# The down projection of a decoder layer in seven products of quarters, with GpSimd forming the operand sums

## The reference, cut to what matters

```python
h2 = _rmsnorm(x, g_pre_ffn)
ffn = (jax.nn.silu(h2 @ w_gate) * (h2 @ w_up)) @ w_down      # (1032, 2816) @ (2816, 1024)
x = x + _rmsnorm(ffn, g_post_ffn)
```

## Time and profile before

| | us |
|---|---|
| median of 3 runs | 1290.61 (1289.73 to 1292.06) |
| the profiled execution | 1288.78 |
| its span, first to last instruction | 1286.9 |
| TensorE busy | 1244.6 |
| VectorE busy | 838.0 |
| ScalarE busy | 465.4 |
| GpSimd busy | 37.2 |

### The profile page before, as it was taken

One profiled execution on the slowest core, in us unless ns is written; L12 is line 12 of the kernel. 1 busy time (PEld: TensorE's weight loads), 2 busy tenths in 40 slices (PEclk: granted clock), 3 DMA queues, 4 the chain that ended last, 5 costly groups with the idle time before them and its releaser, 6 DMA issues.

```text
span 1286.9 us, 22506 instructions
## 1 busy us (share of the span) xinstructions
PE 1244.6 (97%) x9161; PEld 1221.6 (95%) x9161; DVE 838.0 (65%) x1476; ACT 465.4 (36%) x910; POOL 37.2 (3%) x52
## 2 busy tenths in 40 slices
...
GB/s 290 102 70 50 33 19 2 42 11 85 17 69 49 101 110 121 67 98 138 94 108 94 128 54 87 65 94 99 50 88 79 150 330 176 117 251 180 103 274 109
DMA packets 141877, 135.29 MB, mean 105 GB/s; under 512 B 15976, under 2 KB 124792, under 8 KB 141248
## 3 DMA queue, kind: packets, MB, share of 16 engines
...
## 4 chain that ended last, share of the span: by engine, by line
PE 57%; DVE 8%; issue 1%; ACT 1%; DMA 0%; POOL 0%; POOLq 0%; DVEq 0%; ACTq 0%
PE pair L1495 32%; PE pair L1533 16%; PE pair L1454 5%; PE pair L1224 1%; DVE w_lo L2113 1%; DVE mix L1963 1%; PE pair L1353 1%; DVE mix L1988 1%; DVE w_lo L1921 1%; DVE qinv L1959 1%; DMA raw<-w_down_dram 0%; PE pair L1420 0%; DVE yo L2134 0%; POOL yo L840 0%; ACT w_hi L846 0%
## 5 line engine op out<-in xcount | busy, mean ns | idle before, releaser
L1495 PE MATMUL pair<-act_hi,w_hi 128*128 128x258 f32 x704 | 199.6, 284 | 4.3 <-DVE w_lo L1921 2.8
L1495 PE MATMUL pair<-act_hi,w_lo 128*128 128x258 f32 x704 | 198.9, 283 | 0.0
L1495 PE MATMUL pair<-act_lo,w_hi 128*128 128x258 f32 x704 | 198.8, 282 | 0.0
L1224 PE MATMUL pair<-act_hi,w_hi 128*128 128x344 f32 x528 | 180.4, 342 | 6.4 <-DVE act_lo L1586 3.5
L1533 PE MATMUL pair<-h_hi,w_hi 128*128 128x400 f32 (+1 forms) x528 | 170.4, 323 | 1.7 <-DVE h_lo L2116 1.7
L1224 PE MATMUL pair<-act_hi,w_lo 128*128 128x344 f32 x528 | 171.6, 325 | 0.0
L1224 PE MATMUL pair<-act_lo,w_hi 128*128 128x344 f32 x528 | 171.5, 325 | 0.0
L1533 PE MATMUL pair<-h_hi,w_lo 128*128 128x400 f32 (+1 forms) x528 | 170.0, 322 | 0.0
L1533 PE MATMUL pair<-h_lo,w_hi 128*128 128x400 f32 (+1 forms) x528 | 169.8, 322 | 0.0
L1495 PE MATMUL pair<-s_hi,w_lo 128*128 128x258 f32 x528 | 149.3, 283 | 0.0
L1495 PE MATMUL pair<-s_hi,w_hi 128*128 128x258 f32 x528 | 149.2, 283 | 0.0
...
## 6 DMA issues: line engine op xcount, KB each, us to landing
...
hraw<-h_scratch SPq DMA_DIRECT2D x44, 200.0 KB, 4.0
...
```

What stands on the lines that cost most here:

```text
L1224: mm = pe.matmul(out, a[:, k, :], b[:, k, cols(c)], start=(k == 0 and s == 0), stop=(k == KT - 1 and s == 2))
L1495: mm = pe.matmul(pair[psum_pair(n)][:, s, 0:QW], a[:, r, half + k, :], b, start=(k == 0 and i == 0), stop=(k == 3 and i == 2))
```

## The change

The down projection becomes seven products M1 to M7, each of half the rows (516), half the inner width (11 tiles) and half the output width (512), in the order M3, M1, M7, M5, M4, M2, M6 (`DOWN`). `A_OF` and `B_OF` say which quarters of h and of w_down are added or subtracted for each. Their outputs are added into the four quarters of the output.

A step loads, sums, splits and multiplies one inner tile: 4 output tiles x 2 blocks of 258 rows x 3 matmuls. All eight banks belong to each product, two per output tile (`dpair`). M6 runs its two row blocks one after the other, so it has 22 half-steps of 12 matmuls.

The four quarters h11, h22, w11 and w22 stay on chip after their first load, and so does w12 + w11, formed in M4 and split there and in M6's first steps (`TURN_AT`). In M3 a step loads h11, w12 and w22 (770 KB), in M1 h22 and w11, in M7 h12 and w21, in M5 h12, in M4 w21 and w12, in M2 h21, in M6 the half row block of h21. The loads wait as before for the split three before; M6 has six input slots.

The operand sums are GpSimd's (`sum_b`, `sum_a`), and so are most residual sums (`add_x2`, two tiles of 258 columns at once). In the tail GpSimd adds the residual to 5 of 8 tiles and VectorE to 3. Products are taken out of PSUM by copies on ScalarE (`y_copy`) and by copies and adds on VectorE (`y_first`, `y_add`), `y_add` having one operand in PSUM, one in SBUF. The wait for the stores of h to land goes from SyncE's queue to `holes_stored` on ScalarE and VectorE.

The core of the diff; the removed lines of the functions printed above are left out:

```diff
-DCH = ((0, 400), (400, 400), (800, 232))
 DR, DH = 3, 4
-HELD = 3
+HELD = 4
+POOL_TAIL = 5
+ADD, SUB = ALU.add, ALU.subtract
+DOWN = ("M3", "M1", "M7", "M5", "M4", "M2", "M6")
+A_OF = {"M1": ("11", "22", ADD), "M2": ("21", "22", ADD), "M3": ("11",), "M4": ("22",), "M5": ("12", "11", ADD),
+        "M6": ("21", "11", SUB), "M7": ("12", "22", SUB)}
+B_OF = {"M1": ("11", "22", ADD), "M2": ("11",), "M3": ("12", "22", SUB), "M4": ("21", "11", SUB), "M5": ("22",),
+        "M7": ("21", "22", ADD)}
+STEPS = [(p, m) for p in DOWN[:-1] for m in range(HALVES)] + [("M6", m) for _ in range(2) for m in range(HALVES)]
+FULL = (len(DOWN) - 1) * HALVES
+AT = {p: HALVES * i for i, p in enumerate(DOWN)}
+TURN_AT = {AT["M4"] + 3 + m if m < 8 else FULL + m - 8: m for m in range(HALVES)}
...
+    a_ring, _ = at("a_ring", [P, DH, 2, HALF], F32R, region)
+    b_ring = [(w_hi[:, (2 + n) % 4, 0:4].rearrange("p k n -> p (k n)"), w_lo[:, (2 + n) % 4, 0:4].rearrange("p k n -> p (k n)"))
+              for n in range(DH)]
...
+    b_in = [rawx[:, i // 2, 4 * (i % 2):4 * (i % 2) + 4].rearrange("p k n -> p (k n)") for i in range(DR)]
...
+    HALF_SLOT = [max(v for v in range(FULL) if v % DH == n) for n in range(DH)]
+    def a_free(v):
+        if v < DH:
+            return prod_used("P6" if v < 2 else "P7")
+        if v < FULL:
+            return step_used(v - DH)
+        h = v - FULL
+        return step_used(v - 2 * DH) if h >= 2 * DH else step_used(HALF_SLOT[h // 2])
...
+        def load_a(v):
+            p, m = STEPS[v]
+            slot, name = a_slot(v)
+            if p == "M4":
+                return
+            if v >= FULL + DR and v < FULL + 2 * DR:
+                sp.wait_ge(sem("d_split"), FULL)
+            elif v >= FULL + 2 * DR:
+                sp.wait_ge(sem("h_split"), v - 2 * DR + 1)
+            elif v >= DR:
+                sp.wait_ge(sem("h_split"), v - DR + 1)
+            if p == "M3":
+                sp.wait_ge(*prod_used("P1" if m < 4 else "P2" if m < 8 else "P5"))
+                load_h(a11(m), m, "11", name)
+            elif p == "M1":
+                load_h(a22(m), m, "22", name)
+            elif p == "M6":
+                load_h(slot, m, "21", name, slice(QW * sub(v), QW * sub(v) + QW))
+            else:
+                load_h(slot, m, A_OF[p][0], name)
...
+        for v in range(DR, NSTEP):
+            if v == AT["M1"]:
+                sp.wait_ge(sem("prod"), NPROD)
+                sp.wait_ge(sem("hid"), HIDDEN_AT["21", FT - 1])
+            load_a(v)
+            if v < FULL:
+                load_w(v)
+            k = v - (AT["M2"] + DR + 1)
+            if 0 <= k < KT:
+                sp.wait_ge(sem("a_sum"), a_sums(AT["M2"] + k + (k >= 4)))
+                sp.dma_start(x2a(k, 1)[:, 0], x2_d[:, k, HALF:ROWS]).then_inc(sem("x2_in"), 16)
+            if v == FULL + 10:
+                sp.wait_ge(sem("x2_in"), 16 * KT)
+                sp.wait_ge(sem("acc_mm"), 4 * (len(DOWN) - 1))
+                for k in range(0, KT, 4):
+                    sp.dma_start(x2b[:, k:k + 4], x2_d[:, k:k + 4, 0:HALF]).then_inc(sem("x2_in"), 16)
+            if v == FULL + 14:
+                for k in range(0, KT, 2):
+                    sp.wait_ge(sem("y_done_p"), KT // 2 + k // 2 + 1)
+                    sp.dma_start(t_out["y_cols"][:, k:k + 2, HALF:ROWS], yo[:, k:k + 2, HALF:ROWS]).then_inc(sem("y_out"), 16)
...
+        def sum_b(v):
+            p, m = STEPS[v]
+            if not b_summed(v):
+                return
+            pool.wait_ge(sem(B_SEM[v % DR]), b_count[v])
+            x = b_in[v % DR]
+            if p == "M1":
+                pool.wait_ge(sem("d_split"), v - DR + 1)
+                pool.tensor_tensor(x, b11(m), b22(m), ADD).then_inc(sem("b_sum"), 1)
+                return
+            if p == "M4":
+                pool.tensor_tensor(t_in32[:, m], t_in32[:, m], b11(m), ADD)
+            y = b11(m) if B_OF[p][1] == "11" else b22(m)
+            pool.tensor_tensor(x, x, y, B_OF[p][2]).then_inc(sem("b_sum"), 1)
+        def sum_a(v):
+            p, m = STEPS[v]
+            if not a_summed(v):
+                return
+            x, name = a_slot(v)
+            pool.wait_ge(sem(name), a_count[v])
+            if p == "M1":
+                pool.wait_ge(sem(f"rows_in{m % DR}"), a_count[m])
+                pool.wait_ge(sem("h_split"), v - DR + 1)
+                pool.tensor_tensor(x, a11(m), a22(m), ADD).then_inc(sem("a_sum"), 1)
+                return
+            y = a11(m) if A_OF[p][1] == "11" else a22(m)
+            pool.tensor_tensor(x, x, own(y, v), A_OF[p][2]).then_inc(sem("a_sum"), 1)
+        def add_x2(b, k, n=2):
+            rows = block_rows(b)
+            x = yo[:, k:k + n, rows]
+            r = QW * (b % 2)
+            y = x2a(k, n)[:, :, r:r + QW] if b < 2 else x2b[:, k:k + n, r:r + QW]
+            pool.wait_ge(sem("y_t"), KT * b + k + n)
+            pool.tensor_tensor(x, x, y, ADD).then_inc(sem("y_done_p"), 1)
+        for v in range(NSTEP):
+            if v == AT["M1"]:
+                pool.wait_ge(sem("hid"), HIDDEN_AT["21", FT - 1])
+            if v < FULL:
+                sum_b(v)
+            sum_a(v)
+            n = v - (FULL - 3)
+            if 0 <= n < 8:
+                if n == 0:
+                    pool.wait_ge(sem("x2_in"), 16 * KT)
+                add_x2(n // 4, 2 * (n % 4))
+        pool.wait_ge(sem("x2_in"), 16 * (KT + 2))
+        for k in range(0, KT, 2):
+            add_x2(2, k)
+        for k in range(POOL_TAIL):
+            add_x2(3, k, 1)
...
         def down_hi(v):
+            p, m = STEPS[v]
+            if v < FULL:
+                if b_summed(v):
+                    act.wait_ge(sem("b_sum"), b_sums(v))
+                act.wait_ge(*b_free(v))
+                copy(b_ring[v % DH][0], b_source(v)).then_inc(sem("d_hi_done"), 1)
+            if v in TURN_AT:
+                t = TURN_AT[v]
+                act.wait_ge(sem("b_sum"), b_sums(AT["M4"] + t))
+                copy(t_hi(t), t_in32[:, t])
+            if a_summed(v):
+                act.wait_ge(sem("a_sum"), a_sums(v))
+            elif p == "M3":
+                act.wait_ge(sem(f"rows_in{v % DR}"), a_count[v])
+            act.wait_ge(*a_free(v))
+            copy(a_tile(v, 0), a_source(v)).then_inc(sem("h_hi_done"), 1)
...
+        for v in range(2, NSTEP):
             down_hi(v)
+            if v == AT["M1"] + 2:
+                holes_stored(act)
+                y_copy("M3")
+                act.activation(rstd[:, 0:1], eps[:], ACT.Sqrt)
+            if v == AT["M7"] + 2:
+                y_copy("M1")
+            if v == AT["M4"] + 4:
+                y_squares("12", 0)
+                y_squares("12", 1)
+            if v == AT["M2"] + 2:
+                y_copy("M4")
+                y_squares("11", 0)
+                y_squares("11", 1)
+            if v == AT["M2"] + 3:
+                y_root(0)
+                y_root(1)
+            if v == FULL + 2:
+                y_copy("M2")
+            if v == FULL + 5:
+                y_squares("21", 0)
+                y_squares("21", 1)
+            if v == FULL + HALVES + 2:
+                y_squares("22", 0)
+            if v == FULL + HALVES + 5:
+                y_root(2)
+        y_squares("22", 1)
+        y_root(3)
...
+        def down(v, mt, s):
+            p, m = STEPS[v]
+            cut = slice(P * mt, P * mt + P)
+            if v < FULL:
...
+            for n, (b, a) in enumerate(((bh, ah), (bh, al), (bl, ah))):
+                mm = pe.matmul(dpair(mt)[:, s, 0:QW], b[:, cut], a, start=(m == 0 and n == 0), stop=(m == HALVES - 1 and n == 2))
+            return mm
+        def tile_step(v, mt):
+            p, m = STEPS[v]
+            if m == 0:
+                pair_taken(v, mt)
+            for s in range(2) if v < FULL else (sub(v),):
+                mm = down(v, mt, s)
+            if m == HALVES - 1:
                 mm.then_inc(sem("acc_mm"), 1)
+            elif mt == 3:
                 mm.then_inc(sem("down_mm"), 1)
 
+        def pair_taken(v, mt):
+            if v == 0:
+                pe.wait_ge(sem("ffn_read"), READ_AT[vector_reads(NPROD - 4 + mt)[-1]])
+            elif v <= FULL:
+                p = DOWN[v // HALVES - 1]
+                if p in ("M3", "M1", "M4", "M2"):
+                    pe.wait_ge(sem("y_cp"), COPY_AT[p, mt])
+                pe.wait_ge(sem("y_ev"), ADD_AT[p, {"M3": "22", "M1": "22", "M7": "11", "M5": "12", "M4": "11", "M2": "22"}[p], mt])
+        def y_stat(b, out):
+            pe.wait_ge(sem("y_sum"), (3, 4, 7)[b])
+            pe.matmul(out[:, 0:QW], ones[:], ysum[:, b % 2], start=True, stop=True).then_inc(sem("y_stat"), 1)
+        for v in range(NSTEP):
+            p, m = STEPS[v]
+            if v < FULL:
+                pe.wait_ge(sem("d_split"), v + 1)
             pe.wait_ge(sem("h_split"), v + 1)
+            held = p == "M2" and m < HELD
+            for mt in range(3 if held else 4):
+                tile_step(v, mt)
```

(138 more changed lines are left out.)

344 lines of the change are left out of this document (173 added, 171 removed).

## The result

The changed kernel takes 1317.75 us (1313.24 to 1318.56, 4 runs) against 1290.61 us for the kernel before: 1.0202 times as long, 95% interval 1.0177 to 1.0227. It is 2.0% slower, 27 us; the forecast was 1280.5 us, 0.8% faster, and 1317.75 lies outside its range (1262 to 1303).

The account below looks back on a forecast made before the run. The bound moves from TensorE to VectorE and GpSimd's shared path for 33 steps. Matmuls of 221.0 us plus 28.7 make the stage 249.7, 9.1 less; tail 1.0 less: 1290.6 - 10.1 = 1280.5 us, range 1262 to 1303.

Parts of the forecast that it names:

- the price of a pair: Down projection steps: a VectorE split (0.54 us) and a GpSimd sum (1.13 us) alternate, 1.67 us together.
- Rival A: Down projection: GpSimd works ahead, so exclusion costs nothing; stage 227.3 us, some 1256 us in all; chance 0.12.
- Rival B: Down projection: exclusion without overlap, 1.87 us a pair, sign turning at about 1.76; 1293 to 1303 us; chance 0.30.
- M3: First product: step 3's loads land in 3.9 us, sum and splits take 2.5; +0.5 us.
- M1 and M7: Second and third products: vector side starts some 4 us ahead, then needs 3.34 us a step; +5.9 us.
- M5: Fourth product: no lead left, the eviction stands behind this product's third split; +4.3 us.
- M4: Fifth product: lead of 6.7 us, splits at 3.34 or 3.88 us a step, eight adds, two trees; +5.5 us.
- M2: Sixth product: eviction behind the third split, +5 us; reciprocals, scalings and output sums between the splits, +2.5 us.
- M6: Last product: eviction behind the third half-step's delayed split, 3.4 us, and GpSimd's output sums, 1 more; +4.4 us.
- rival C: Input ring of three slots sets the pace, deciding above a landing of 5.5 us; 1306 us; chance 0.08.
- Statistics matmuls between steps: +0.6: Down projection: statistics matmuls placed between the steps add 0.6 us to the stage.
- Tail: From the last matmul to the end: 13.0 us against 14.0 before, -1.0 us.

Follow-up runs that it names:

- e5: The changed kernel with four input slots in place of three and GpSimd's residual sums three steps later; 1300.09 us, 1.0090 times the kernel before.
- e7: e5 with each of GpSimd's operand sums cut to 8 columns, so the output is not the reference's; 1267.61 us.
- e2: The changed kernel with four input slots in place of three; 1308.09 us, 1.0152 times the kernel before.
- e3: The changed kernel with GpSimd's first residual sums started three steps later; 1312.13 us, 1.0177 times the kernel before.
- e4: The changed kernel with all operand sums on VectorE, one step ahead of their splits, residual sums still on GpSimd; 1309.09 us, 1.0138 times the kernel before.
- e6: e5 with the operand sums of M3 to M2 on VectorE, those of M6 still on GpSimd; 1280.63 us, 0.9935 times the kernel before.

## Why the prediction was wrong

The mechanism and the price of a pair were right: the sums exclude the splits at 1.71 us a pair (1.67 taken). What failed is how waits arise from it and what a wait costs. Rival A's hidden sums are refuted by both time lines. Rival B's price, 1.87, is not what is seen, and its threshold of 1.76 was not reached; yet the time came out beyond B's. The stage was put at 249.7 us and took 284.0, 34.3 more. 16.8 of these are the lower clock behind the waits, some 14 are longer waits (41.9 us against 28.1), and some 4 statistics matmuls and short gaps. By the prediction's own terms, each over 31.6 us of matmuls:

| term | predicted | after | e5 | e7 |
|---|---|---|---|---|
| M3 | 0.5 | 8.4 | 1.3 | 0.0 |
| M1 and M7 | 5.9 | 15.5 | 15.0 | 0.2 |
| M5 | 4.3 | 0.7 | 0.0 | 0.0 |
| M4 | 5.5 | 10.5 | 9.7 | 2.1 |
| M2 | 7.5 | 18.6 | 10.7 | 3.3 |
| M6 | 4.4 | 9.1 | 11.9 | 10.2 |

- **M3, "landing 3.9 us, sum and splits 2.5", the step that failed first.** From step 3's first issue to its last split it took 11.7 us. The load that its sum waits for landed after 5.2 us, was issued 2.0 us behind the first, and sum and splits took 4.4. With three slots each round waits for that. This is rival C's mechanism, near its own point of 5.5 us, but in M3 alone, where a step has three loads: 7.9 us over the term, of which e2 gives back 6.4 and e5 7.1 (3 us less if e3's M3 is the measure). The 3.9 us is the median of 41 loads of h in the kernel before. Its trace holds the warning: the 11 of them issued from 1019 to 1050, among larger loads, have a median of 6.6 us to landing, the 30 after that 3.9.
- **M1 and M7, "some 4 us ahead", and the eviction left out.** The prediction has its first split of M1 4 us before M3 ends. In after it ended at 1057.41, M3's last matmul at 1057.28: no lead. But e5 shows that this is not the main thing. There M3 takes 32.9 us, its last matmul ends at 1046.97 and M1's first pair of splits at 1045.45, 1.5 us before it. VectorE in e5, from M3's last split of h through M1's first three to the eviction:

```profile
1040.23 1.79 DVE L2425 TENSOR_TENSOR a_ring<-act_lo,a_ring 128x516 fp32r<-128x516 f32 x1
...
1043.66 1.79 DVE L2425 TENSOR_TENSOR a_ring<-a_in,a_ring 128x516 fp32r<-128x516 f32 x1
...
1047.06 1.76 DVE L2425 TENSOR_TENSOR a_ring<-a_in,a_ring 128x516 fp32r<-128x516 f32 x1
...
1050.42 1.76 DVE L2425 TENSOR_TENSOR a_ring<-a_in,a_ring 128x516 fp32r<-128x516 f32 x1
1052.10 2.49 DVE L2451 COPY mix<-pair 128x516 f32<-128x516 f32 x4
```

  TensorE waits 6.0 us for that copy. The prediction had this eviction wait, behind the third split, for M5, M2 and M6 but let M1 and M7 pass on the lead. Its own numbers give it 3.3 us at M1 even with the 4 us: 2 x 3.34 + 0.6 - 4. The stop gives the vector side its lead back, and the waits of M1, M7 and M5 come to 12.0 us in after (6.5, 4.9 and 0.6) and 10.8 in e5, where the terms have 10.2. The other 4.0 us in each are slower matmuls. A longer ring of input slots (e2, e5) helps loads, and M1 needs split operands.
- **M2, a wait not in the sum.** GpSimd's residual addition stood ahead of an operand sum and waited 10.1 us for its loads; e3 gives back 7.6 us in M2, but M6 takes 3.9 more. M2's waits are 10.8 us, and 5.7 us of slower matmuls follow them. The trace of before couldn't show it, but the order in the diff did.
- **Slow matmuls, not in the sum.** Every stall was priced at its own length. In after, 41.9 us of waits brought 16.8 us of lower clock with them, 0.4 us for one. In e5 it is 10.6 us for 33.3, worked out in the same way, 0.3 for one. Had the 28.7 us of the prediction been marked up by 0.4, the stage would have been put at 261 us, level with the kernel before.
- **M4 and M6.** M4's waits are 6.0 us (5.5 predicted for the whole term), and 3.9 us of slower matmuls follow them. M6's waits are 6.6 us where the term has 4.4. The first is the 3.5 foreseen, but the last two, 0.8 and 2.3 us, come in every kernel but e4 (there 2.5 and 2.7), e7 too: VectorE's eight scalings of the third block stand between the last splits, beside GpSimd's residual sums, and the groups of four take 2.7 and 3.7 us where four take 1.7 in e6 at 1202.71, with GpSimd idle. The prediction gave this 1 us.
- **"Statistics matmuls between steps: +0.6".** In e7, the kernel with the fewest waits, 236.9 - 221.0 leaves 15.9 us: 9.0 of waits, 3.0 of lower clock after two of them, and 3.9 us of statistics and short gaps, 1.5 of these in M4. The term was some 3 us too small.
- **M5 is 3.6 us better than predicted.** TensorE had been stopped for 4.9 us at M7's start, so the splits were ahead again by its end, and M5's eviction wait is 0.6 us. The prediction lets such a stop refill the ring only after M5.
- **Tail.** 13.0 predicted, 14.7 measured. The scalings and sums took 6.65 us (1305.86 to 1312.51; 6.45 predicted) and the reciprocal 1.76 (1.78). From the last matmul to the reciprocal's end it took 4.7 us where the terms give 3.7, and from the last sum to the end 3.3, not 2.85.

Together these bring a forecast of -10 us to +27. The sums themselves, exclusion and all that follows from it, are 32.9 us of the stage (e5 against e7), the ring and the early additions 14.2 (after against e5). By the accounts of e5 and e7 24.3 of the 32.9 are waits (33.3 against 9.0) and some 7.6 slower matmuls (10.6 against 3.0). No kernel here kept the clock up while the waits stayed, so that the second comes from the first is argued from their order in time, not shown by an experiment. GpSimd's residual sums stay in every kernel here, so their own price is not separated either. e6, with the sums on VectorE, is the test of the cause on a whole computation: its stage is 17.5 us shorter than e5's.
